# Query, key and value projections of two stick-breaking layers as three products of rounded halves

## What is computed

```python
def stick_breaking_attention(h, w_in, w_out):
    """A[t,s] = sigmoid(z_ts) * prod_{s<j<t} (1 - sigmoid(z_tj)), s < t; o_t = sum_s A[t,s] v_s."""
    q, k, v = jnp.split(h @ w_in, 3, axis=-1)        # 256x1024 @ 1024x3072, 16 heads of 64
    ...
        z = jnp.einsum('bhqd,bhkd->bhqk', qb, k) * scale
        later = lax.cumsum(log_keep, axis=3, reverse=True) - log_keep
        a = jnp.where(past, jnp.exp(log_beta + later), 0.0)
        return jnp.einsum('bhqk,bhkd->bhqd', a, v)
    ...
    return merge_heads(o) @ w_out
```

## Time and profile before

| | us |
|---|---|
| median of 3 runs | 2224.56 (2224.03 to 2225.19) |
| the profiled execution, its own time | 2226.48 |
| its span, first to last instruction | 2224.5 |
| mean granted TensorE clock, share of full | 0.959 |
| PE busy | 1998.6 (90%) |
| DVE busy | 784.0 (35%) |
| ACT busy | 679.8 (31%) |
| mean transfer rate | 248 GB/s |

### The profile page before, as it was taken

The page is one execution under the profiler, slowest core; times in us unless marked ns, Lnnn a source line. Parts: engine busy times, 40 slices in busy tenths (PEclk is TensorE's granted clock), DMA queues, the critical chain, the costliest instruction groups (busy, mean ns, idle before and its releaser), DMA issues.

```text
span 2224.5 us, 39741 instructions
## 1 busy us (share of the span) xinstructions
PE 1998.6 (90%) x17230; PEld 1698.4 (76%) x17230; DVE 784.0 (35%) x1397; ACT 679.8 (31%) x1202; POOL 34.5 (2%) x53
## 2 busy tenths in 40 slices
PE   6999867776766899999999999998699999999999
PEld 4788544444443688999977799996489998889999
DVE  1123311101110123545434554543654442235454
ACT  3011200000000324434323344433344443334343
POOL 0000000000000000000000000000000000000000
PEclk9999898899899899999999999999899999999999
DMA  9555799999999825755652565554275466334543
GB/s 389 195 224 224 287 426 428 428 427 428 428 427 427 330 96 204 276 186 185 241 227 89 224 265 189 213 212 192 74 285 208 165 244 253 114 114 150 178 149 130
DMA packets 41003, 552.21 MB, mean 248 GB/s; under 512 B 4545, under 2 KB 4929, under 8 KB 5057
## 3 DMA queue, kind: packets, MB, share of 16 engines
q1 hardware_dynamic: 33984, 449.98, 51.3%
q0 software_dynamic: 6912, 100.67, 11.0%
HBM read 549.58 MB, written 1.05 MB: 248 GB/s over the span
## 4 chain that ended last, share of the span: by engine, by line
PE 74%; DMA 18%; DVE 3%; ACT 3%; issue 1%; SPq 0%; DVEq 0%
PE bank L407 39%; DMA ring<-in_moe 17%; PE bank L394 10%; PE bank L401 5%; PE bank L464 4%; PE bank L676 3%; PE bank L386 2%; PE bank L449 1%; PE bank L441 1%; PE bank L859 1%; PE bank L476 1%; DMA ring<-in_ada_head 1%; PE bank L775 1%; ACT work L1199 1%; PE bank L794 0%
## 5 line engine op out<-in xcount | busy, mean ns | idle before, releaser
L407 PE MATMUL bank<-xsq_parts,ring_parts 128*128 128x256 f32 x1408 | 399.7, 284 | 0.0
L407 PEld LDWEIGHTS bank<-xsq_parts,ring_parts 128*128 128x128 f32 x1408 | 271.6, 193 | 0.0
L394 PE MATMUL bank<-hT,ring 128*128 128x256 f32 x1024 | 235.7, 388 | 3.0 <-DVE mod L1509 1.8
L676 PE MATMUL bank<-ring,xsq 128*32 128x256 f32 x2048 | 145.6, 433 | 100.0 <-DMA ring<-in_moe 99.1
L394 PEld LDWEIGHTS bank<-hT,ring 128*128 128x128 f32 x1024 | 195.0, 193 | 37.2 <-issue 7.7
L1004 ACT CAST mixT_parts<-ring 128x1024 fp32r<-128x1024 f32 (+1 forms) x152 | 151.7, 1003 | 191.8 <-PE bank L407 191.8
L407 PE MATMUL bank<-xsq_parts,mixT_parts 128*128 128x256 f32 x704 | 201.8, 287 | 3.0 <-DVE hT_parts L1393 2.8
L407 PE MATMUL bank<-hT_parts,mixT_parts 128*128 128x256 f32 x704 | 200.4, 285 | 0.0
L676 PEld LDWEIGHTS bank<-ring,xsq 128*32 128x32 f32 x2048 | 67.0, 121 | 173.9 <-DMA ring<-in_moe 127.7
L407 PE MATMUL bank<-hT_parts,xn_parts 128*128 128x256 f32 x704 | 199.2, 283 | 0.0
L407 PE MATMUL bank<-xsq_parts,xn_parts 128*128 128x256 f32 x704 | 199.2, 283 | 0.0
(11 more groups left out here) (314 smaller groups left out, 3506.4 us busy)
## 6 DMA issues: line engine op xcount, KB each, us to landing
ring<-in_moe SPq DMA_DIRECT2D x96, 2048.0 KB, 12.5
ada_ring<-in_ada POOLq DMA_DIRECT2D x48, 2048.0 KB, 12.2
ring<-in_gu SPq DMA_DIRECT2D x44, 2048.0 KB, 8.1
ring<-in_down SPq DMA_DIRECT2D x32, 1408.0 KB, 6.2
ring<-in_pair SPq DMA_DIRECT2D x24, 1536.0 KB, 6.6
ring<-in_na SPq DMA_DIRECT2D x12, 2048.0 KB, 9.6
ring<-in_out SPq DMA_DIRECT2D x10, 2048.0 KB, 8.2
ring<-in_ada_head SPq DMA_DIRECT2D x3, 2048.0 KB, 16.4
```

Source lines behind the costliest of these rows:

```text
L394: m = mm(dst, w[:, k, lo:lo + P], h[:, k, :], start=k == 0, stop=k == KT - 1)
L407: m = mm(dst, w[a], x[b], start=start and (a, b) == (0, 0), stop=stop and a == 1)
L676: m = mm(bank[0][CAP * q:CAP * (q + 1), 0:T], xg[:, 4 * c + k, h * CAP:(h + 1) * CAP], w[:, k, q * T:(q + 1) * T], start=(c, k) == (0, 0), ...
```

## The change

In the stick-breaking layers all three projections are made with `split_product`. `normalise` gives way to `normalise_split`, so that `xsq` and `hT` hold the halves of the input. Each pair's three weight tiles (query, key, value) are split: ScalarE casts them with `cast_pair` into three buffers `w_pair_hi`, which belong to the output projection otherwise, and VectorE subtracts with `low_pair`. Pair 0's are split around the norm. During step s those of pair s + 1 are cast: query after the copy of query and key, key after the last exponential, value after the value product of pair s; VectorE subtracts query and key ahead of its copy of the values, and the value tile in step s + 1 behind the masked scores. TensorE waits on `attn_lo` ahead of each tile. `out_hi` and `out_lo` become `attn_hi` and `attn_lo`, with counts that allow for the added splits. Moba and swa layers are as before but for these counts.

```diff
@@ tensor: sb_pair
                     if not last:
-                        wait_chunk(pe, n, r)
-                        w = chunk3(n, 3 * P)
-                        project(bank[0][:, 0:T], w, 0, hT, x0 if first else None)
-                        project(bank[0][:, T:2 * T], w, P, hT).then_inc(sk["qk_proj"], 1)
+                        for f in range(2):
+                            pe.wait_ge(attn_lo, pair_splits(i) + 3 * step + f + 1 + 3 * RING * r)
+                            for k in range(KT):
+                                if first and f == 0:
+                                    pe.wait_ge(h_lo, split_norms(i, False) + k + 1)
+                                m = split_product(bank[0][:, f * T:(f + 1) * T], (w_pair_hi[f][:, k, :], part["w_pair"](n, f)[:, k, :]),
+                                                  (part["xsq"][:, k, :], part["hT"][:, k, :]), k == 0, k == KT - 1)
+                        m.then_inc(sk["qk_proj"], 1)
...
                     if not last:
                         pe.wait_ge(sk["v_ready"], j)
-                        rows(bank[1][:, 0:T].rearrange("p (t n) -> p t n", t=TT), w, 2 * P, P, hT).then_inc(used[n % RING], 1)
+                        pe.wait_ge(attn_lo, pair_splits(i) + 3 * step + 3 + 3 * RING * r)
+                        for t in range(TT):
+                            for k in range(KT):
+                                m = split_product(bank[1][:, t * P:(t + 1) * P], (part["xsq"][:, k, t * P:(t + 1) * P], part["hT"][:, k, t * P:(t + 1) * P]),
+                                                  (w_pair_hi[2][:, k, :], part["w_pair"](n, 2)[:, k, :]), k == 0, k == KT - 1)
+                        m.then_inc(used[n % RING], 1)
...
@@ scalar: ahead of the pairs, and sb_pair
+                def cast_pair(step, r, f):
+
+                    if f == 0:
+                        wait_chunk(act, n0 + step, r)
+                    copy(w_pair_hi[f], full["w_pair"](n0 + step, f)).then_inc(attn_hi, 1)
...
+                norm(4 + 2 * i, xT, ready, hT, gcol(0), scol(mod, 0), first_pair if split_h else None, split_h or None)
+                if split_h:
+                    act.wait_ge(h_lo, split_norms(i, False) + 4)
+                    cast_pair(0, 0, 2)
...
+                    following = not last and step + 1 < PAIRS
                     if not last:
                         act.wait_ge(sk["qk_proj"], j + 1)
                         copy(qk[:, :], bank[0][:, :]).then_inc(sk["qk_ready"], 1)
+                    if following:
+                        cast_pair(step + 1, r, 0)
                     if not first:
                         act.wait_ge(sk["w_ready"], j)
                         A(probT_l[:, :, 0:TRI], prob_l[:, 2:4, 0:TRI], ACT.Exp).then_inc(sk["a_ready"], 1)
                         if last:
                             cast_out(0, 1)
+                    if following:
+                        cast_pair(step + 1, r, 1)
+                        wait_used(act, n0 + step, r)
+                        cast_pair(step + 1, r, 2)
+                    if not first:
                         act.wait_ge(sk["o_done"], j)
...
@@ vector: ahead of the pairs, and sb_pair
+                def low_pair(step, r, f):
+
+                    dve.wait_ge(attn_hi, pair_splits(i) + 3 * step + f + 1 + 3 * RING * r)
+                    V.tensor_tensor(part["w_pair"](n0 + step, f), full["w_pair"](n0 + step, f), w_pair_hi[f].bitcast(F32),
+                                    ALU.subtract).then_inc(attn_lo, 1)
+
+                if KINDS[i] == "sb":
+                    for f in range(2):
+                        low_pair(0, 0, f)
+                    normalise_split(4 + 2 * i, split_norms(i, False), 0, 0)
+                    low_pair(0, 0, 2)
+                else:
+                    normalise(4 + 2 * i)
...
                         m.then_inc(sk["zm_ready"], 1)
+                        if not last:
+                            low_pair(step, r, 2)
                         dve.wait_ge(sk["ln"], j)
...
+                    if not last and step + 1 < PAIRS:
+                        for f in range(2):
+                            low_pair(step + 1, r, f)
                     if not last:
                         values(sk, step, r, j, first)
```

More of the change, by code:

```diff
@@ L158, in split_views @@
             v["w_gu"] = lambda n, f: ring[n % RING][:, :].rearrange("p (k n) -> p k n", k=KT)[:, :, f * P:(f + 1) * P]
+            v["w_pair"] = lambda n, f: ring[n % RING][:, 0:3 * KT * P].rearrange("p (k n) -> p k n", k=KT)[:, :, f * P:(f + 1) * P]
             v["w_down"] = lambda n, f: ring[n % RING][:, parts[f] * P:parts[f + 1] * P]
@@ L171, in build @@
         w_out_hi = [t[:, :, :] for t in w_out_hi] + part["whi"][2:4]
+        w_pair_hi = (w_out_hi[1], w_out_hi[0], part["whi"][2])
         htok = flat(xn).rearrange("p (t d) -> p t d", t=TT)
@@ L231, in build @@
                              "e_turned", "e_taken", "y_taken", "y_spread"))
-        out_hi, out_lo, o_low = (sem(n) for n in ("out_hi", "out_lo", "o_low"))
+        attn_hi, attn_lo, o_low = (sem(n) for n in ("attn_hi", "attn_lo", "o_low"))
         w_hi, w_lo, h_hi, h_lo, f_hi, f_lo, tile_done = (
@@ L313, in norm_bank, with pair_splits, out_splits, split_norms @@
             return bank[4 if e == 2 or e > 4 and e % 2 else 3]
+        def pair_splits(layer):
+            return 8 * layer + 3 * PAIRS * sum(KINDS[i] == "sb" for i in range(layer))
+        def out_splits(layer):
+            return pair_splits(layer) + 3 * PAIRS * (KINDS[layer] == "sb")
+        def split_norms(layer, ffn):
+            return KT * (layer + sum(KINDS[i] == "sb" for i in range(layer + ffn)))
         def epoch(layer):
@@ L422, in out_proj @@
                             pe.wait_ge(mods_taken, g + 1)
-                        pe.wait_ge(out_lo, 8 * i + 4 * c + f + 1)
+                        pe.wait_ge(attn_lo, out_splits(i) + 4 * c + f + 1)
                         for k in range(KT):
@@ L754, in _ @@
                 group_rows(4 * i + 2, "attn")
-                x0 = KT * (4 + i)
+                x0 = KT * (4 + i - sum(KINDS[l] == "sb" for l in range(i)))
                 n0 = FIRST.get(f"pair_{i}")
@@ L957, in gate_up @@
                             if (step, f) == (0, 0):
-                                pe.wait_ge(h_lo, KT * i + k + 1)
+                                pe.wait_ge(h_lo, split_norms(i, True) + k + 1)
                             dst = bank[2 * s + f // 2][:, f % 2 * T:(f % 2 + 1) * T]
@@ L1153, in _, with first_pair @@
                 act.wait_ge(mods_ready, 3 + 2 * i)
-                norm(4 + 2 * i, xT, ready, hT, gcol(0), scol(mod, 0))
+                n0 = FIRST.get(f"pair_{i}")
+                def cast_pair(step, r, f):
+                    if f == 0:
+                        wait_chunk(act, n0 + step, r)
+                    copy(w_pair_hi[f], full["w_pair"](n0 + step, f)).then_inc(attn_hi, 1)
+                def first_pair():
+                    for f in range(2):
+                        cast_pair(0, 0, f)
+                split_h = KINDS[i] == "sb"
+                norm(4 + 2 * i, xT, ready, hT, gcol(0), scol(mod, 0), first_pair if split_h else None, split_h or None)
+                if split_h:
+                    act.wait_ge(h_lo, split_norms(i, False) + 4)
+                    cast_pair(0, 0, 2)
                 group_out(4 * i + 2, "attn")
@@ L1162, in cast_out @@
                         wait_chunk(act, n)
-                    copy(w_out_hi[f], full["w_gu"](n, f)).then_inc(out_hi, 1)
+                    copy(w_out_hi[f], full["w_gu"](n, f)).then_inc(attn_hi, 1)
                 def sb_pair(step, r, first=False, last=False):
@@ L1325, in _ @@
                 for f in range(2, 4):
-                    act.wait_ge(h_lo, KT * i + 4 * (f - 1))
+                    act.wait_ge(h_lo, split_norms(i, True) + 4 * (f - 1))
                     split(0, 0, f)
@@ L1637, in _ @@
             for i in layers:
-                normalise(4 + 2 * i)
                 n0 = FIRST.get(f"pair_{i}")
@@ L1644, in low_out @@
                     n = FIRST[f"out_{i + 1}"] + c
-                    dve.wait_ge(out_hi, 8 * i + 4 * c + f + 1)
+                    dve.wait_ge(attn_hi, out_splits(i) + 4 * c + f + 1)
                     V.tensor_tensor(part["w_gu"](n, f), full["w_gu"](n, f), w_out_hi[f][:, :, :].bitcast(F32),
-                                    ALU.subtract).then_inc(out_lo, 1)
+                                    ALU.subtract).then_inc(attn_lo, 1)
                 def low_mix(k, j, at):
@@ L1870, in _ @@
                     split(0, 0, f)
-                normalise_split(5 + 2 * i, KT * i, 2, 3 * KT)
+                normalise_split(5 + 2 * i, split_norms(i, True), 2, 3 * KT)
                 for f in range(2, 4):
```

1 line of the change is left out of this document (added).

## The result

The changed kernel takes 2226.97 us (median of 20 runs, 2223.00 to 2234.38), the kernel before beside it 2222.78 us (20 runs, 2220.25 to 2225.85). The ratio is 1.0023, 95% interval 1.0014 to 1.0031: slower by 5.1 us (0.0023 x 2222.78), between 3.1 and 6.9 (the two medians lie 4.2 apart). Forecast were +10.1 us, twice as much. Two later groups of runs of the same kernel gave 1.0023 and 1.0018. The kernel before came out 1.8 us faster over 20 runs than over the 3 that the forecast of 2234.7 started from, so the differences are what to compare.

The account below looks back on a forecast made before the run. It took the pair loops to be bound by TensorE alone. Query and key -20.2, values +29.4 and norm +0.9 made +10.1 us on the median 2224.56, so 2234.7 us; the range was 2224 to 2285.

Parts of the forecast that it names:

- Query and key: Pair loops: 48 rounded-half instructions at 0.1198 take 5.75 us for 7.01, gaining 1.26 a pair, 20.2 in 16.
- Values: Pair loops: 48 load-limited instructions at 0.1147 take 5.51 us for 3.67, losing 1.84 a pair, 29.4 in 16.
- The steady step: Pair loop: 14.7 us for 14.10 (5.75 query and key, 5.5 values, the rest 3.4), no idle on TensorE.
- The splits: Casts on ScalarE and subtractions on VectorE, 3.0 and 3.7 us a pair, fit into idle time: cost 0.
- The norm ahead of pair 0: TensorE waits some 0.45 us for the eighth low half, 0.9 us in two layers; between 0 and 1.5.
- The step behind pair 0: Step after pair 0 in each stick-breaking layer: the sum put its growth at +0.58 us.
- the last line of the sum: Whole kernel: +10.1 us added to the profiled 2226.48 for 2236.6, and to the median 2224.56 for 2234.7.
- rival C: Clock falls in the value stretch, +24 to +45 us: 2258 to 2280; chance 0.12.
- Rival A: Value loop: rounded instructions cost only their columns, 0.0574 us each, so the kernel is faster, 2190.6; chance 0.09.
- Rival B: Value loop: short rounded products take full-precision passes, 0.2190 us each, +90 us, 2314.8; chance 0.11.
- Rival D: Pair steps: a split comes late, 1 to 2 us a step in 14 steps, 2249 to 2263; chance 0.02.

Follow-up runs that it names:

- the two half-sized kernels: Changed kernel with value products of 64 moving columns instead of 128, or of 64 stationary positions instead of 128: 2278.41 us and 2187.95 us, one run each.
- The kernel with 25 idle products: Kernel before plus 25 unread full-precision 128x128 products per stick-breaking layer, into an otherwise idle bank: ratio 1.0016 (1.0007 to 1.0026).

## Why the prediction was right and wrong

**Query and key: right.** 5.75 us forecast, 5.81 measured. Done alone they brought 1.21 us a step for the forecast 1.26.

**Values: right, and for the reason given.** 5.51 forecast, 5.49 measured. Inside the stretch the spacing is 0.111, at the lower end that I read from the few-column products of the earlier trace rows. That 48 times 0.1147 fits so closely is in part luck: the rest comes from the two ends of the stretch, 0.15 from the first product to the second and 0.21 from the last to the attention. That the load sets it was an argument from the earlier trace rows; the two half-sized kernels show it. Alone, values cost 1.74 a step for the forecast 1.84.

**The steady step.** 14.7 forecast, 14.63 measured. The rest of it came out 0.08 shorter than before, in the suffix products (1.67 for 1.75), so the step grew by 0.53 and not by 0.58.

**The splits: right.** No idle on TensorE in the step, with VectorE and ScalarE busy for 7.27 and 7.17 us of 14.63. The sum that the suffix products wait for ends 4.9 us into the step (808.75 + 0.96 - 804.82), 0.9 ahead of them, as forecast.

**The norm ahead of pair 0: wrong, small.** Forecast 0.45 us of waiting a layer. In the first loop TensorE waits once, before the step behind pair 0, as it did before the change:

```profile
PE bank L421 <- DVE mod L1556: 0.5, 1, 0.5
```

The stretch up to the first scores grew from 10.68 to 11.20 us, 0.52, which is the extra work of a pair alone. No late half was met, because the last ones come faster than I read from the first five in the earlier trace rows. VectorE's last three are one run, 0.40 apart:

```profile
761.01 1.27 DVE L1440 SCALAR_TENSOR_TENSOR hT_parts<-xn,mod,xsq_parts 128x256 fp32r<-128x256 f32 x3
```

The eighth is there at 762.28; TensorE, which began with query at 760.11, comes to it at 762.6.

**The step behind pair 0.** 16.03 for 15.78 (790.85 - 775.07), +0.25 where the sum put +0.58. It holds the half-clock stretch of the earlier trace rows in both kernels, and query and key, which meet it, gained 1.48 us there (8.69 to 7.21) for 1.20 in a steady step.

So the loops: forecast 9.2 + 0.9 = 10.1, measured 8.1. Two of the missing five microseconds are the terms above: 0.9 of the norm, some 0.5 in the 12 steady steps, some 0.6 in the two behind pair 0.

**The step that failed is the last line of the sum**: "2226.48 + 10.1" and "2224.56 + 10.1". It adds the growth of the loops to a whole run, as though every stage in which no line changed kept its time. It has no term for them and no width. Measured is 5.1, so the outside gave back 3.0 by the 20 runs of each kernel, between 1.2 and 5.0 (8.1 in the one traced pair, which happened to be far apart). The runs showed in its place a term of -4 to +4 us for the half-clock stretches of stages that do the same work as before, and here it was as large as a third of the effect. The kernel with 25 idle products gave back as much, so a later start without any split is enough for it, to the 2 us or so of that measurement; what in a later start decides it stays open. The earlier trace rows had it in sight: I read there what one fall of the clock costs (1.69 us) and used it for rival C alone, not for the many falls in the stages behind.

The sign held, for the reason given, and so did the range. The size did not: 0.23% measured for 0.45% forecast, and the interval, 0.14 to 0.31%, does not clear the 0.2% that I had called tellable. That 2226.97 lies in the range is no merit of it: its low part stood for cheaper values or no wait in the norm, and values cost what was forecast. Above, with rival C in it, the range was far too wide.

**Rival A** (values become short) falls: 0.11 and not 0.057, by the change itself and by the kernel with 64 moving columns. The Trainium skill, page "TensorE: Matmul & The Clock Gate", section "Weight-path perf modes", switches its fast load on for 128 weights of a type other than FP32; the rounded type has 128 here and loads in the same 193 ns and at the same 0.11 spacing as the unrounded, so here it counts as FP32, or the fast load is not on, or gives nothing; the runs do not tell these apart. **Rival B** falls: no spacing of 0.219 anywhere. **Rival C** did not come, the granted clock is 1.00 in the steady steps; but at 64 moving columns it comes in every step. **Rival D** falls with the idle time.

## What to carry to other kernels

Where a stationary load of 128 columns stands behind every product, count loads, not passes: three rounded halves for one full-precision product pay at 256 moving columns (3 x 0.12 for 2 x 0.22 us) and lose at 128 (3 x 0.11 for 2 x 0.115), and the way out is a wider moving side, not fewer splits. Split a change that touches both into its halves before it is judged: +5.1 us here was -22.9 and +28.0. And when a change of 0.4% is read in a kernel of 2.2 ms, the other stages can move the whole by 0.2% of their own, so cut the trace into the part that changed and the rest, and put a control beside it that only shifts the start.

## What the runs showed of the hardware

- Rounded products with a 128x128 stationary: spacing 0.12 us at 256 moving columns, 0.111 at 128, 0.11 at 64; with 64 stationary and 128 moving columns 0.060.
- The granted clock is at its higher level through the steady steps with 5.5 us of 128-column products in each, and it goes to the lower (0.50 of 2.4 GHz) for 3 to 10 us in or just behind each such stretch of 64-column ones, with the same number of instructions at the same spacing and, in the steady steps, no idle time.
- The changed kernel took the time between its two loops in 987.8, 988.2 and 991.8 us, in three executions, and the difference is in how much of it TensorE worked at the lower clock.
